# Two more projections of a two-block transformer kernel computed from rounded halves, their weights rounded by GpSimd alone, with merged gate sums; one weight group of the next stage rounded early

## The reference, cut to what matters

```
u = modulate(rms_norm(h), ...)                  # 512 latent + 256 context tokens
# layer 0 ("even")
z = u @ w_in_even                               # 1024 -> 2496: q, k, v, gate, a, b, MLA downs
q, k, v = silu(short_conv(z[qkv], 5 taps));  q, k = l2_normalize per head
g = -exp(a_log) * softplus(a + dt_bias);  beta = sigmoid(b)        # 32 columns of z
a_out = gated delta rule over chunks, both directions;  b_out = MLA attention
y = concat(a_out, b_out) @ w_out_even           # 1024 -> 1024, all 768 tokens
# layer 1 ("odd")
z = u @ w_in_odd ...
```

## Time and profile before

| what | value |
|---|---|
| median of 3 runs | 3546.45 us (3540.0 to 3550.61) |
| profiled execution | 3542.84 us, span 3541.0 us, mean granted clock 0.968 |
| PE / DVE / ACT / POOL busy | 94% / 47% / 35% / 31% of the span |
| even, normalization to the last projection product | 1313.0 to 1563.3 us |
| even_out, projection | 2060.7 to 2145.4 us |
| odd, wait between opening and m-tile 2 | 2770.2 to 2780.4 us |

### The profile page before, as it was taken

The page is one execution under the profiler, slowest core; times in us unless marked ns, Lnnn a source line. Parts: engine busy times, 40 slices in busy tenths (PEclk is TensorE's granted clock), DMA queues, the critical chain, the costliest instruction groups (busy, mean ns, idle before and its releaser), DMA issues.

```text
span 3541.0 us, 43752 instructions
## 1 busy us (share of the span) xinstructions
PE 3314.6 (94%) x17864; PEld 2529.3 (71%) x17864; DVE 1679.0 (47%) x3140; ACT 1234.8 (35%) x2211; POOL 1106.6 (31%) x933
## 2 busy tenths in 40 slices
PE   7999999887899999989889998999999898999998
PEld 3346888655688875655678866888887677868886
DVE  7744446598466676414556624122223318731223
ACT  2413233347432235225523214212113336843222
POOL 0233444551244430011165402222222342034443
PEclk9999999999999999989999999999999999999999
DMA  7514555210255551100122120111111111012222
GB/s 298 190 74 164 205 209 198 106 48 1 73 212 210 210 207 48 48 25 1 40 49 55 47 77 31 72 69 51 72 51 69 54 48 66 1 48 99 103 102 78
DMA packets 82408, 337.17 MB, mean 95 GB/s; under 512 B 46432, under 2 KB 50208, under 8 KB 57376
## 3 DMA queue, kind: packets, MB, share of 16 engines
q1 hardware_dynamic: 81344, 332.14, 25.2%
q10 hardware_dynamic: 864, 2.24, 0.2%
HBM read 326.64 MB, written 7.70 MB: 94 GB/s over the span
## 4 chain that ended last, share of the span: by engine, by line
PE 78%; DVE 11%; ACT 4%; POOL 2%; DMA 2%; issue 2%; SPq 1%; POOLq 0%; DVEq 0%; ACTq 0%
PE PSB L644 16%; PE PSB L648 16%; PE PSB L645 15%; PE PSB L559 12%; PE PSB L1238 2%; PE PSB L1260 2%; PE PSB L1247 2%; DVE SB L392 1%; DVE SB L1332 1%; DMA SB<-in_ada 1%; PE PSB L1799 1%; DVE SB L1348 1%; DVE PSB L986 1%; DVE SB L1643 1%; DVE R L992 1%
## 5 line engine op out<-in xcount | busy, mean ns | idle before, releaser
L648 PE MATMUL PSB<-R,WSR 128*128 128x512 f32 (+1 forms) x2700 | 915.7, 370 | 0.0
L617 POOL TENSOR_TENSOR WSR<-SB,ahead 128x1024 fp32r<-128x1024 f32 x183 | 438.6, 2398 | 715.0 <-ACT ahead L594 714.9
L644 PE MATMUL PSB<-R,ahead 128*128 128x512 f32 (+1 forms) x1672 | 615.6, 368 | 10.2 <-POOL WSR L617 10.1
L645 PE MATMUL PSB<-R,ahead 128*128 128x512 f32 (+1 forms) x1672 | 595.7, 366 | 0.0
L648 PEld LDWEIGHTS PSB<-R,WSR 128*128 128x128 f32 x2700 | 473.8, 189 | 65.8
L559 PE MATMUL PSB<-SB 128*128 128x512 f32 (+1 forms) x1312 | 479.6, 527 | 7.6 <-ACT SB L1458 6.2
L559 PEld LDWEIGHTS PSB<-SB 128*128 128x128 f32 x1312 | 253.0, 193 | 232.3 <-issue 213.4
L644 PEld LDWEIGHTS PSB<-R,ahead 128*128 128x128 f32 x1672 | 314.5, 188 | 81.7 <-POOL WSR L617 11.8
L645 PEld LDWEIGHTS PSB<-R,ahead 128*128 128x128 f32 x1672 | 314.6, 188 | 53.4 <-issue 0.7
L617 POOL TENSOR_TENSOR WSR<-SB,ffn_weights 128x1024 fp32r<-128x1024 f32 x96 | 230.1, 2397 | 389.4 <-ACT ffn_weights L594 389.4
L644 PE MATMUL PSB<-R,ffn_weights 128*128 128x512 f32 x868 | 324.4, 374 | 8.2 <-POOL WSR L617 8.2
(11 more groups left out here) (400 smaller groups left out, 5072.7 us busy)
## 6 DMA issues: line engine op xcount, KB each, us to landing
SB<-in_w SPq DMA_DIRECT2D x95, 2048.0 KB, 7.8
SB<-in_ada SPq DMA_DIRECT2D x96, 1024.0 KB, 5.2
SB<-gate_rows SPq DMA_DIRECT2D x12, 512.0 KB, 4.0
SB<-in_rpb SPq DMA_DIRECT2D x8, 448.0 KB, 3.8
spill<-SB SPq DMA_DIRECT2D x1, 3072.0 KB, 9.6
SB<-gate_rows SPq DMA_DIRECT2D x24, 128.0 KB, 3.9
SB<-spill SPq DMA_DIRECT2D x1, 3072.0 KB, 9.8
SB<-in_x SPq DMA_DIRECT2D x8, 256.0 KB, 6.5
```

Of the source, the lines that this page charges most:

```text
L617: e.tt(lr, t, hf, ALU.subtract).then_inc(*G.up(("lo", self.e0 + j)))
L644: e.mm(b[:, 0:n], wh, xh[:, lo:lo + n], x == 0, False)
L645: e.mm(b[:, 0:n], wh, xl[:, lo:lo + n], False, False)
L648: ins = e.mm(b[:, 0:n], wl, xh[:, lo:lo + n], False, last)
```

## The change

The whole of `even`'s input projection and of `even_out`'s is computed from halves. In `even` ACT rounds groups 0 and 1 during ffn1's end, and POOL makes their rests before `after`; all later groups are rounded and subtracted by POOL (`pool_alone`), into three buffers, the third in the context region XCR, free once the normalization has read it. The pads move into X's region, so ACT's first evacuation and POOL's fills wait for `h` 15 and for the spill, and POOL handles group 2 ahead of the fills. The 32 gate columns become the stationary side: 8 k times 2 chunks times 3 products of 32 output rows, an ACT copy, and 6 transposes after m-tile 14. The gate sums become three products of 48, 48 and 96 columns. In `even_out` ACT and DVE split the eight inputs into halves first, MLA's four ahead of the delta rule's, and ACT and POOL round the weights. In `odd` group 2 gets a buffer of its own; ACT rounds groups 2 and 3 between the two chunks of the normalization, POOL subtracts ahead of its fills. `norm_halves_*`, `HeadNorm`, mla and gdn stay as they are, apart from where tiles lie.

```diff
-    stat("e_out", 8, 8)
+    while len(plan) % GROUP:
+        plan.append(None)
+    for m in range(8):
+        plan.extend(("e_out", k, m) for k in E_OUT)      # E_OUT = (4, 5, 6, 7, 0, 1, 2, 3)
...
+            def pool_alone(self, e, G, j):
+                p, t, (hf, hr, lr) = self.group(j)
+                e.wait_ge(*W.landed(p))
+                if j >= len(self.bufs):
+                    e.wait_ge(*self.st.at("group_used", self.e0 + j - len(self.bufs)))
+                e.cp(hr, t).then_inc(*G.up(("hi", self.e0 + j)))
+                self.pool(e, G, j)
...
+        class WithThird(HalvesInPlace):
+            def group(self, j):
+                p, t, (_, _, lr) = super().group(j)
+                hf, hr = self.bufs[j] if j < 2 else self.third if j == 2 else self.bufs[(j - 3) % 2]
+                return p, t, (hf, hr, lr)
+            def act(self, e, A, j):
...
+                    if j >= 3:
+                        e.wait_ge(*self.st.at("group_used", j - 3 if j < 5 else j - 2))
+                    e.act(hr, t, ACT.Copy).then_inc(*A.up(("hi", j)))
...
# ffn1, act, last quarter
+                            if i == 1 and mt >= 6:
+                                ahead_act(e, "even", mt - 6)
...
# even, pe
-                        g = linear(e, st, g, ring, "e_in", [mt], 8, H, BOTH, pre2_ready(st))
+                        g = linear3(e, st, g, ring, hv, "e_in", [mt], range(8), H, BOTH, ready)
+                    if mt == 14:
+                        gate_columns_pe(e)
...
+                for c, (lo, n) in enumerate(BOTH):
+                    e.wait_ge(*st.at("head_ln", 7, c))
+                for k in range(8):
+                    wh, wl, j, used = hv.take("e_in", k, 20)
+                    e.wait_ge(*st.at("lo", j))
+                    _, xh, xl = H[k]
+                    for c, (lo, n) in enumerate(BOTH):
+                        ps = banks[6 + c][0:32, 0:n]
+                        e.mm(ps, wh[:, 0:32], xh[:, lo:lo + n], k == 0, False)
+                        e.mm(ps, wh[:, 0:32], xl[:, lo:lo + n], False, False)
+                        ins = e.mm(ps, wl[:, 0:32], xh[:, lo:lo + n], False, k == 7)
...
+            def gate_columns_pe(e):
+                e.wait_ge(*st.at("ab_read", 1))
+                for b in range(6):
+                    e.tr(banks[6][:, 32 * b:32 * b + 32], ABR[:, col(b)], ident[0:32, 0:32]).then_inc(*P.up(("ab_sum", b)))
...
+                for d, tri in enumerate(("triF", "triB")):
+                    e.mm(by_direction(banks[7][:, 0:96], d), K[tri], by_direction(GG, d))
+                e.mm(banks[7][:, 96:192], ones, GG).then_inc(*P.up(("g_sums",)))
...
# even, act: the copy ABR <- banks 6, 7 comes at mt == 12, the read of ab_sum at mt == 14 (was 13)
-                pre2_act(e, A, st, m, 0, H, True)
+                norm_halves_act(e, A, st, S, H, 0, m[0][0], banks[4:6], 0)
+                norm_halves_act(e, A, st, C, H, S, m[0][1], banks[4:6], 8)
+                e.wait_ge(*st.at("h", 15))
+                e.wait_ge(spill_landed, 16)
...
# even, pool
+                for j in range(2):
+                    hv.pool(e, G, j)
+                after(e, st)
+                e.wait_ge(*st.at("h", 15))
+                e.wait_ge(spill_landed, 16)
+                hv.pool_alone(e, G, 2)
                 (8 fills of the pads)
+                for j in range(3, hv.groups):
+                    hv.pool_alone(e, G, j)
...
# even_out
-                linear(e, st, 0, ring, "e_out", range(8), 8, MIX, BOTH, lambda k, lo: [])
+                g = opening3(e, st, ring, hv, [("e_out", 0), ("e_out", 1)], 8, MIX, BOTH, ready, E_OUT)
+                linear3(e, st, g, ring, hv, "e_out", range(2, 8), E_OUT, MIX, BOTH, ready)
...
+                for x in range(8):
+                    if x < 2:
+                        hv.act(e, A, x)
+                    e.act(MIX[x][1], mixed[x], ACT.Copy).then_inc(*A.up(("mixed_hi", x)))
+                hv.act(e, A, 2)
...
+                for x in range(8):
+                    v.wait_ge(*st.at("mixed_hi", x))
+                    v.tt(MIX[x][2], mixed[x], MIX[x][0], ALU.subtract).then_inc(*D.up(("mixed", x)))
...
+                for j in range(8):                       # even_out, pool, ahead of the wait for the spill
+                    hv.pool(e, G, j)
...
# odd, act: between norm_halves_act of the latent and of the context chunk
+                hv.act(e, A, 2)
+                hv.act(e, A, 3)
...
# odd, pool: ahead of the waits for the rope and for h 15; the later loop starts at 4
+                hv.pool(e, G, 2)
+                hv.pool(e, G, 3)
```

More of the change, by code:

```diff
@@ L663, in opening3 @@
                     for i, (name, mt) in enumerate(tiles_):
[L664 removed]
+                        wh, wl, j, used = sp.take(name, ks[x], mt)
                         _, xh, xl = xs[x]
@@ L1842, in even @@
             QKV, GT = tiles(12, ST), tiles(4, ST)
-            MIXb = alloc(8 * ST)
-            H = [MIXb[:, f * ST:(f + 1) * ST] for f in range(8)]
+            MIXb = SB[:, pos[0]:pos[0] + 8 * ST]
+            H = pairs(8, ST)
             RAW = tiles(4, ST)
@@ L1847, in even @@
             mark = pos[0]
-            PADS = tiles(2, 776)
-            cw, gl, gc = small(60), small(8), small(8)
-            hn = HeadNorm(st, lambda i: BOTH, banks[6:8], 1.0, lambda i: 0.125 if i < 4 else 1.0, QKV[0:8],
-                          tiles(3, ST), tiles(2, ST))
+            WS = [rounded_tiles(f"even_weights{j}", 1, GROUP * 128, -(-pos[0] // 64) * 64 + j * GROUP * 128)[0] for j in range(2)]
+            pos[0] = -(-pos[0] // 64) * 64 + 2 * GROUP * 128
+            cw, gl, gc = small(60), small(8), small(8)
+            hv = next_weights["even"] = HalvesInPlace(st, [t for t in W.plan if t and t[0] == "e_in"], WS)
+            after_weights, pos[0] = pos[0], x0
+            PADS = tiles(2, 776)
+            HQ = tiles(3, ST)
+            assert pos[0] <= xc0
+            WS.append((XCR[:, 0:GROUP * 128].bitcast(F32), XCR[:, 0:GROUP * 128]))
+            pos[0] = xc0 + GROUP * 128
+            HR = tiles(1, ST)
+            assert pos[0] <= x0 + 8 * ST
+            pos[0] = after_weights
+            HR += tiles(1, ST)
+            hn = HeadNorm(st, lambda i: BOTH, banks[6:8], 1.0, lambda i: 0.125 if i < 4 else 1.0, QKV[0:8], HQ, HR)
+            ABR = HQ[0][0:32, :]
             ring = (0, 1, 2, 3, 4, 5)
@@ L1887, in gate_inputs_pe @@
             def gate_inputs_pe(e):
-                for b in range(6):
[L1889 to L1895, removed]
+                for c, (lo, n) in enumerate(BOTH):
[9 more added lines that the diff above has]
+                        ins = e.mm(ps, wl[:, 0:32], xh[:, lo:lo + n], False, k == 7)
+                        done = ([("ab_row", c)] if k == 7 else []) + (used if c else [])
+                        if done:
+                            ins.then_inc(*P.up(*done))
+            def gate_columns_pe(e):
+                e.wait_ge(*st.at("ab_read", 1))
+                for b in range(6):
+                    e.tr(banks[6][:, 32 * b:32 * b + 32], ABR[:, col(b)], ident[0:32, 0:32]).then_inc(*P.up(("ab_sum", b)))
             def gate_sums_pe(e):
@@ L3083, in odd @@
             NG = len(groups)
-            hv = next_weights["odd"] = HalvesInPlace(st, [t for t in W.plan if t and t[0] in ("o_in", "nav", "gv")], AHEAD)
+            third = rounded_tiles("odd_weights", 1, GROUP * 128, keys_at + 6 * ST)
+            hv = next_weights["odd"] = WithThird(st, [t for t in W.plan if t and t[0] in ("o_in", "nav", "gv")], AHEAD, third[0])
             value_bank = lambda b: (NG + b) % 6
@@ L3231, in pool @@
                     e.wait_ge(*G.now())
-                for j in range(2, 12):
+                for j in range(4, 12):
                     hv.pool(e, G, j)
```

60 lines of the change are left out of this document (44 added, 16 removed).

## The result

The changed kernel takes 3500.63 us (median of 4 runs, 3495.86 to 3505.76) against 3545.95 (4 runs, 3540.0 to 3550.61) of the kernel before beside it: ratio 0.9865, 95% interval 0.9848 to 0.9883, 45.3 us faster. The forecast was 3514, with a range of 3480 to 3540. The profiled execution took 3505.76 us, span 3503.9, mean granted clock 0.967: 37.1 us less than that of before.

What follows compares the result with a forecast made beforehand. TensorE was taken to bound the kernel, in even by less than a microsecond per tile. 3542.84 - 12 (even) - 9 (even_out) - 9 (odd) = 3512.8, stated as 3514 us; forecast band 3500 to 3530, range 3480 to 3540.

Steps and rivals of the forecast that it cites:

- rival A: In even, GpSimd's work falls into VectorE's waits: even gains 47 us, 3474 in all (3500 where half hidden); chance 0.23.
- Pace of the products: New products in even and even_out: k step 1.053 us against 1.290, so an m-tile falls from 10.32 to 8.43.
- Steps (1) to (3): Even's start: GpSimd block about 1.3 us, opening 20.6, TensorE waits 2 for group 2, VectorE starts at 1338.0.
- Step (4): Even's first tile: VectorE and GpSimd take turns until 1356.1, only then TensorE's head norm 0; 4.1 us late.
- Step (5): Even's next cycles: 13.3 us each (10.7 to 16.6), GpSimd released into VectorE's context half; norm 7 at 1448.4, 15.1 lost.
- Step (6): Even after head norm 7: TensorE waits before the gate transposes; 103 us to the end (96 to 110), 27 gained.
- Even in sum: Net gain of the even stage: 27 - 15 = 12 us (from -14 to 47).
- mla and gdn move earlier as they are: The stages between even and even_out only start earlier, with no term of their own in the sum.
- B: In even, worst turns of VectorE and GpSimd in every cycle, 16.6 us: even loses 14, 3546 in all; chance 0.12.
- C: In even, TensorE's clock falls to about half after idle gaps past about 4 us: 3575 in all; chance 0.05.
- Signs: Expected in even: k step 1.05 us, VectorE operations 1.7 to 3, TensorE idle 2 to 5; odd's wait 2 to 3.

Runs made afterwards that it cites:

- cut: Changed kernel, but in even GpSimd casts 16 columns twice for groups 3 to 20 instead of casting and subtracting 1024 (outputs not the reference's); 3485.4 us.
- split4: Changed kernel, but in even GpSimd's cast and subtraction of groups 3 to 20 are each four instructions of 256 columns; 3493.6 us.
- dve_sub: Changed kernel, but in even VectorE makes the subtractions of groups 2 to 10 and GpSimd only casts them; 3487.9 us.
- act_rounds: Changed kernel, but in even ScalarE rounds groups 3 to 20 behind a tile's evacuation and GpSimd only subtracts; 3496.0 us.
- gates_as_moving: Changed kernel, but in even the 32 gate columns, in halves, stay the moving side, without copy or transposes; 3520.1 us.

## Why the prediction was right, and where it missed

The direction and the three parts were right. The time came 13 us lower, at the lower edge of the forecast's band of 3500 to 3530 and at rival A's "to 3500 where half is hidden"; half of the blocking was hidden. Inside, even gained 20 us more than forecast, and mla and gdn, which the forecast had at nothing, gave 7 back. That the sum came as near as it did is partly luck. This is where:

- **Pace of the products.** Right: in the tail, ten m-tiles, the gate tile and small products take 95.6 us without a wait, the forecast's lower bound of 96. Before's 15.63 us of gate columns held 10.4 us at half clock, which the change removed with them. Even_out 10.4 us against 9 forecast, odd 8.0 against 9.
- **Steps (1) to (3).** Right: the block at ffn1's end 1.1 us (1.3); scaling to the opening's end 20.9 (20.6); TensorE's wait for group 2 2.32 (2), first evacuation 1338.00 (1337.3), VectorE 1338.72 (1338.0).
- **Step (4).** Head norm 0 at 1353.95, forecast 1356.1. I added GpSimd's 10 us for three groups to VectorE's own 8.3 and 0.5 (which makes 18.8, not the 18.1 written); they held it 4.7 in the latent convolution (7.81 for 3.11) and 2.1 at the start of the context half (2.42 for 0.35, an operation with one SBUF input), and the rest fell into its waits.
- **Step (5), the step that failed most.** A cycle of 11.9, not 13.3. The release, I had said, falls into the context half, where nothing is slack. It falls at the start of the latent convolution, from 0.03 us before it to 1.65 behind. I had let TensorE start its tile with the loop, at ScalarE's evacuation, as it does in the kernel before. But once the loop sets the pace, the head norm's product waits for ScalarE's Ln of the norm before (L1432), which comes behind the evacuation and a table load: 1387.29 to 1390.19, 2.9 us. The tile then ends 2.9 + 9.7 = 12.6 us or a little more after the loop's start, in the next loop of 11.9. There ScalarE's head norm and table load cover half of the blocking. The mechanism is the forecast's (`cut`: 14.3 us), its place is not. Norm 7 at 1437.47, forecast 1448.4.
- **Step (6).** Tail 95.6, not 103; 34.5 us gained against 27. I counted five m-tiles of TensorE ahead of the gate transposes; there are six (10, 11, 12, the gate tile, 13, 14), so it came 52 us after norm 7, not 43. ScalarE's copy, which I had only behind VectorE's 57 us, was made at 46. No wait.
- **Even in sum.** 32.4 us (253.1 to 220.7), 12 forecast: between the forecast and rival A's 47, somewhat nearer to A. Of the 20.4 us of surplus some 13 are norm 7's (steps 4 and 5) and 7.5 the tail's (step 6).
- **"mla and gdn move earlier as they are."** Wrong by 11 us in the profiled pair, by 6.8 in the means (492.6 of three profiles, 499.4 of eleven). It took back a third of even's surplus over the forecast: 32.4 - 6.8 + 10.4 + 8.0 = 44.0, of 45.3 measured.
- **Rivals.** B's turns of 16.6 did not come. C's half clock came, but briefly: after head norm 0, behind 7.58 us of idling, the clock was 0.55 for 4 us; in a later cycle, behind 1.78, it was 0.79 for 8 us, and TensorE was still back ahead of the loop. C's condition, gaps past about 4 us, was too high: idling of 1.78 and 1.87 us was followed by a fall, another of 1.76 by none. It cost time in gdn and at odd's m-tile 4, where 2.39 us of idling are followed by 4.3 us at a clock of 0.65, 1.5 us more.
- **Signs.** As forecast: the pace, VectorE operations of up to 2.78 us (mean 0.94 over both chunks), odd's wait of 2.39. Not as forecast: TensorE idles 0.2 to 1.9 us before the head norms behind the first, not 2 to 5, and not at all before the gate transposes.

The Trainium skill (SBUF, State Buffer; "Who interferes with whom") was the ground for steps (4) and (5): a VectorE instruction with two SBUF inputs and a GpSimd instruction that reads SBUF exclude each other. The trace agrees for the subtraction (5.75 and 5.08 us beside it, 3.11 without). `split4` refines it: beside four short casts VectorE loses 0.06 us and GpSimd waits, beside four short subtractions both lose (4.48 us for 3.11, and 4.17 for 2.9).

## What to carry to other kernels

Where two engines block each other, price the block only after you have placed it: find what releases the second engine, and whether the first has slack at that point; a wait downstream that another engine fills anyway absorbs it. Before handing an elementwise job to an idle engine, ask what it costs the busy one to do it in its own wait: here 1.22 us of VectorE replaced 2.0 of blocking and was free. A stage that the change doesn't touch is not neutral if its waits are a race that a microsecond decides, as in gdn: compare several profiles before its length goes into a sum. And read the granted clock beside every price that you carry over: the 0.163 us of the old gate columns looked like a price per product, and was a mean of 0.11 and 0.21 at two clocks.

## What the runs showed of the hardware

- GpSimd's 128x1024 cast held VectorE's chain of 128x512 two-input operations 0.67 us (`dve_sub`), its 128x1024 subtraction 2.0 to 2.25 (`act_rounds`); as four pieces of 256 columns the cast held them 0.06 and took 2.81 us itself, the subtraction 1.37 and 4.17 (`split4`).
- VectorE subtracts 128x1024 into fp32r in 1.22 us (`dve_sub`), GpSimd in 2.40 alone and 2.7 beside VectorE's convolution.
- fp32r products of 32 moved columns start every 0.111 us at a granted clock of 1.00 and every 0.213 at 0.50 (`gates_as_moving`), those of 512 every 0.227 at 1.00 (changed kernel, 1322 us).
- In a row of such narrow products without a gap the granted clock fell to 0.50: after 2.4 us in `gates_as_moving`, and after 5.2 to 5.9 us of the float32 passes of before.
- In gdn the granted clock was 0.50 from 1975.40 to 1989.00, from 0.3 us after TensorE had resumed from 1.19 us of idling.
